# First head's values inside its forget product, an expert ring place released by halves, and one scatter moved ahead

## The chip, the core and the metric
The kernel runs on one core of a Trainium2 chip. The time is the device time of one execution in microseconds (us). TensorE (PE) multiplies; its weight loads (PEld) overlap its products. VectorE (DVE), ScalarE (ACT) and GpSimd (POOL) work elementwise, and SyncE (SP) issues most transfers. An engine takes its instructions strictly in the order written, and engines wait for one another on semaphores. PE runs at one of two clocks, 1.2 or 2.4 GHz.

## The reference
One inference layer for 256 prompt frames and 64 sample frames (T = 320 columns), width 1024:

```
x   = LN(x)
h @ w_in -> q, forget logits, values, output gate (8 heads of 128), conv branch, branch gates
logf = log_sigmoid(z) + log1p(lb * exp(-z));  k = (1 - lb) * sigmoid(-z)
S_t = diag(f_t) S_{t-1} + k_t v_t^T;  o_t = S_t^T q_t          per head, chunks of 64
A   = (rms_norm(o) * silu(g)) @ w_o_a
B   = silu(LN(causal depthwise conv(GLU))) @ w_o_b
x   = LN(alpha * x + (sig(ga) * A + sig(gb) * B) @ w_out)
y   = sum over 16 experts: gate_e * ((silu(x @ wg_e) * (x @ wu_e)) @ wd_e)   top 2 of one group of 4
out = LN(alpha * x + y)
```

The outputs are both y, and the new recurrent and conv states.

## The kernel before
**Start.** x is normalised, PE transposes it (L515) to 8 feature slices of 128 x 320 in PSUM. ACT and DVE turn each slice k into three things: xT (f32), a high part xh and a low part xl = xT - xh (both rounded for PE's faster f32 form). `X_COPIES` is DVE's order: "Tk" copies slice k to xT, "Lk" makes xl k. ACT walks k = 0 to 7: a slice that DVE copies needs one ACT instruction (L1108, xh from xT), any other needs two (L1111, L1112). A projection of one head is 24 products of 320 columns: weights high x xh, low x xh, high x xl. The weights' high part is made by ACT (`w_high`, L1076), the low part by DVE (`w_low`, L1568); POOL makes the very first one.

**Heads.** The mixer goes through 8 heads. In its turn each engine handles the current head and the one before it, in the order that its `head_turn` is written in. For the current head: PE makes the forget logits (`cur_f`, for head 0 `first_f`), q (`cur_q`) and values (`cur_v`, three `value_tile`s, plain f32: 24 products that stand as 48 in the trace). ACT runs the forget chain (L1123 to L1129), DVE the scan (L1591 to L1599). DVE and POOL then build 7 levels of decay differences (`level_decay` L1608, `key_decay` L1453), ACT exponentiates all of them in one instruction (`level_exp`, L1157), DVE and POOL multiply in q and k (L1621, L1467), and DVE ends with three small products; the last (L1635) is the decayed key. For the previous head: PE transposes that key (`prev_kT`, L596), makes the block products (`levels`, 64 x 64), the states and the output; DVE masks the block products (`level_mask`, L1644), which it does after the current head's scan and before the current head's level differences. Weights of head n + 2 go over those of head n; SP issues them when head n's values are done (semaphore v_done).

**Experts.** After the mixer x1 (320 rows) is routed. Experts are worked in 8 pairs; a pair has 12 groups of weights of 2 MB: 4 gate, 4 up, 4 down. SP streams them into a ring of 8 places (plus two groups, 11 and 23, kept elsewhere at first). A place is loaded again when PE has counted the old group done (`group_used`). `both` is one group: kk = 0, 1 by two halves of columns by two experts, 8 products of 512 columns (16 in the trace). The columns of a pair's tokens are gathered by PE: 3 products per feature slice (6 in the trace). For the first pair `first_gather(k)` does one slice k; ACT and DVE copy slices out two at a time (L1410, L2050: e.g. slices 0 and 1, semaphore eXT_a 1, and 2 and 3, eXT_b 1), and `first_gate(g)` is gate group g.

**End.** The last pair's down product is cut in quarters of 256 columns: `last_down(c)`, a copy by ACT (L1377), `last_scatter(c)` back to token rows in banks 0 to 2 (c even) or 3 to 5, and an add by DVE (L2067) with statistics (L2091). For the fourth quarter `last_sums` puts the running sum into the banks by PE, and DVE takes its statistics from PSUM (L2101). Then the last LayerNorm and the stores.

Of the kernel before, what the change touches and what calls it, by code (L numbers as in the profile page):

```python
# [25 lines left out]
P = 128  # L26
D = 1024
KT = D // P
# [54 lines left out]
    return c, np.stack(m, 1).reshape(P, LW).astype(np.float32)  # L83


X_COPIES = ("T1", "T3", "L0", "L1", "T6", "L2", "L3", "L4", "L5", "L6", "L7")
ORDER = [2, 0, 1]
X1_BANKS = [6, 7, 4, 5, 0, 1]
LOGIT_BANKS = [6, 7, 4]
# [32 lines left out]
def build(nc, a, o):  # L122
    with ExitStack() as ctx:
# [217 lines left out]
        def _(sp):  # L341
# [38 lines left out]
                sp.dma_start(sob[k], w_ob_k[:, k]).then_inc(wb_in, 16)  # L380
            with sp.Fori(1, 4) as i:
                for b in range(2):
                    sp.wait_ge(h["v_done"], 2 * i + b - 1)
                    load_head(i, b)
                    sp.wait_ge(h["so_ready"], 2 * i + b - 1)
                    sp.wait_ge(h["o_done"], 2 * i + b - 1)
                    load_state(i, b)
# [74 lines left out]
            load_extra(1, (2,))  # L462
            sp.wait_ge(logit_done, 3)
            load_extra(1, (3,))
            for g in range(SLOTS, 4 * PARTS):
                if g not in EXTRA:
                    load_first(g)
            with sp.Fori(2, PAIRS // 2 - 1) as i:
# [36 lines left out]
        def _(pe):  # L505
# [13 lines left out]
            def project(bank, hi, lo):  # L519
# [3 lines left out]
                        last = mm(ps[:, bank, 0:T], w[:, k * P:k * P + P], x[:, k, :], k == 0 and j == 0, k == KT - 1 and j == 2)  # L523
                return last

            def first_f():
                for k in range(KT):
# [4 lines left out]
                for k in range(KT):  # L532
                    pe.wait_ge(xl_ready, XL[k])
                    mm(ps[:, 0, 0:T], wh[:, k * P:k * P + P], xlk[:, k, :], False, False)
                pe.wait_ge(wlo_ready, 1)
                for k in range(KT):
                    last = mm(ps[:, 0, 0:T], wl[:, k * P:k * P + P], xhk[:, k, :], False, k == KT - 1)
                last.then_inc(h["f_done"], 1)

            def cur_f(i, b, first):  # L540
                pe.wait_ge(wlo_ready, 2 * (2 * i + b) + 1)
# [88 lines left out]
            def head_turn(cur, prev, pprev, first=False, first_prev=False):  # L630

                if first:
                    first_f()
                else:
                    cur_f(*cur, first)
                if first or first_prev:
                    cur_q(*cur, first, False)
                if first_prev:
                    prev_kT(*prev, True)
                    levels(*prev, True)  # L640
                    prev_states(*prev)
                if pprev:
                    rms(*pprev)
                    levels(*prev, False)
                    prev_kT(*prev, False)
                    cur_q(*cur, False, True)
                    prev_states(*prev)
                cur_v(*cur, first)
                if prev:
                    prev_out(*prev, first_prev)  # L650

# [177 lines left out]
            def both(bank, lhs, g, first=False):  # L829

                def weights(m, kk):
                    if first and g in EXTRA:
                        return extra[EXTRA.index(g)][2 * m + kk]
                    return wring[:, ring_place(g) % SLOTS if first else slot_of_group(g), m, kk, :]

                for kk in range(2):
                    k = 2 * (g % 4) + kk
                    for hf in range(2):
                        for m in range(2):
                            last = mm(ps[64 * m:64 * m + 64, bank + hf, :], lhs[:, k, 64 * m:64 * m + 64], weights(m, kk)[:, hf * 512:hf * 512 + 512],  # L840
                                      k == 0, k == KT - 1)
                return last

            def group(g, i, first=False):
                if first and g in EXTRA:
                    pe.wait_ge(extra_in[EXTRA.index(g)], 64)
                elif first:
                    pe.wait_ge(group_in[ring_place(g) % SLOTS], 16 * (ring_place(g) // SLOTS) + 16)
                else:
                    pe.wait_ge(group_in[slot_of_group(g)], 16 * (2 * PARTS // SLOTS) * i + 16 * ((g - len(EXTRA)) // SLOTS) + 16)  # L850
# [80 lines left out]
            def last_down(i, b, c):  # L931

                g = PARTS * b + 8 + c
                if c < 3:
                    group(g, i)
                else:
                    pe.wait_ge(e["end_in"], 16)
# [26 lines left out]
            def expert_pair(i, b, begin=False, end=False, first=False):  # L964
# [5 lines left out]
                if end:  # L970
# [30 lines left out]
            for k in range(5):  # L1001
# [4 lines left out]
            first_gather(5)  # L1006
            pe.wait_ge(e["eXT_b"], 1)
            first_gate(1)
            first_gather(6)
            first_gather(7)  # L1010
            pe.wait_ge(e["eXT_a"], 2)
            first_gate(2)
            pe.wait_ge(e["eXT_b"], 2)
# [28 lines left out]
        def _(act):  # L1042
# [172 lines left out]
            def head_turn(cur, nxt, prev, pprev, first=False, first_prev=False):  # L1215
                forget(*cur, first or first_prev)
                if pprev:
                    pprev_rms(*pprev)
                key_exp(*cur)
                if prev:  # L1220
                    prev_states(*prev, first_prev)
                if nxt:
                    w_high(*nxt, 0)
                else:
                    u_high(0, 0)
# [277 lines left out]
        def _(dve):  # L1503
# [170 lines left out]

            def head_turn(cur, nxt, prev, pprev, first=False, first_prev=False):
                forget_in(*cur, first or first_prev)
                if prev:
# [6 lines left out]
                if nxt:  # L1684
                    w_low(*nxt, 0)
                else:
                    u_low(0, 0)
# [314 lines left out]
            def last_hidden(n):  # L2002
                for hf in range(2):
                    cut = slice(hf * 512, hf * 512 + 512)
                    dve.wait_ge(e["group_used"] if hf else e["half_up"], PARTS * n + 8 if hf else 1)
# [156 lines left out]
```

## Time and profile before

| | |
|---|---|
| median of 3 runs | 870.38 us (869.27 to 871.08) |
| profiled execution, its own time | 869.76 us |
| span of that execution | 868.0 us |
| PE busy | 826.0 us, 95% |
| DVE / ACT / POOL busy | 412.5 / 238.2 / 80.0 us |
| HBM read | 247.99 MB |

The span runs from the first to the last instruction; 1.8 us of the execution's time lie around it. Engines share the span unevenly: DVE and ACT are densest in the heads (to about 200 us) and the conv (to about 300 us), while the transfers are saturated only in the expert part, from about 420 us on. A high busy share of PE is therefore no proof that PE sets the end.

### The profile page before, as it was taken

To read this page: it belongs to the slowest core of one execution; us is meant where nothing else is said; L and a number is where in the kernel's file an instruction comes from. 1 tells how busy PE (TensorE), PEld (TensorE's weight loads), DVE (VectorE), ACT (ScalarE), POOL (GpSimd) and SP (SyncE) were. 2 spreads that over 40 slices of the span, in tenths; PEclk is the share of its full clock that TensorE was granted. 3 is DMA by queue.
4 is the path that set the end of the run, shared out by engine and by line. 5 is a ranking of instruction groups with operands and counts; after the bars stand their busy time and mean duration, and the time that the engine had idled before them with its cause. 6 is when DMAs were issued, how large, how long until landed. Compare 5 with 4: busy or idle time off the path is not lost.

```text
span 868.0 us, 12770 instructions
## 1 busy us (share of the span) xinstructions
PE 826.0 (95%) x4976; PEld 536.6 (62%) x4976; DVE 412.5 (48%) x691; ACT 238.2 (27%) x377; POOL 80.0 (9%) x141
## 2 busy tenths in 40 slices
PE   4999999999999999999999999999999999999993
PEld 2989899989999867586353453543535335353351
DVE  6788889988999963876010302103021030210235
ACT  6666655665456415111101010000100001000011
POOL 1344455430000000000000000000000000000000
PEclk9999999999999999999999999999999999999997
DMA  8222222254343712499899999999999999999981
GB/s 317 74 83 84 82 82 82 106 181 148 145 146 123 318 45 103 185 400 413 327 429 430 426 429 427 427 428 427 427 428 430 428 427 430 425 431 424 430 362 62
DMA packets 32006, 251.07 MB, mean 289 GB/s; under 512 B 4638, under 2 KB 8094, under 8 KB 19674
## 3 DMA queue, kind: packets, MB, share of 16 engines
q1 hardware_dynamic: 29424, 249.17, 70.3%
q10 hardware_dynamic: 2538, 1.32, 0.5%
q8 instruction: 28, 0.46, 0.2%
q14 instruction: 16, 0.13, 0.0%
HBM read 247.99 MB, written 2.48 MB: 289 GB/s over the span
## 4 chain that ended last, share of the span: by engine, by line
PE 59%; DVE 21%; ACT 9%; DMA 8%; issue 2%; ACTq 1%; DVEq 0%
PE ps L507 58%; DVE ar L1730 5%; DMA ring<-in_w_down_end 4%; DMA ring<-in_w_gate_e 4%; DVE ring L1608 4%; DVE split_t L1737 3%; ACT ring L1157 2%; ACT ar L1167 1%; DVE ar L1644 1%; ACT split_w L1076 1%; DVE ar L1655 1%; DVE ar L1599 1%; PE ps L881 1%; ACTq L1206 1%; ACT ar L1129 1%
## 5 line engine op out<-in xcount | busy, mean ns | idle before, releaser
L507 PE MATMUL ps<-ring,ar 128*64 128x512 f32 (+1 forms) x1088 | 226.8, 568 | 4.3 <-ACT ar L1361 3.3
L507 PEld LDWEIGHTS ps<-ring,ar 128*64 128x64 f32 x1088 | 88.5, 137 | 130.3 <-issue 120.6
L507 PE MATMUL ps<-ring,xT 128*64 128x512 f32 (+2 forms) x896 | 161.1, 458 | 2.8 <-DMA ring<-in_w_gate_e 2.8
L507 PEld LDWEIGHTS ps<-ring,xT 128*64 128x64 f32 (+1 forms) x896 | 85.9, 152 | 72.8 <-issue 67.1
L2019 DVE TENSOR_TENSOR ar<-ar,ps 128x512 f32<-128x512 f32 (+1 forms) x42 | 28.8, 685 | 214.6 <-PE ps L507 214.5
L507 PE MATMUL ps<-split_x,split_t 128*128 128x320 f32 x672 | 101.0, 310 | 0.5 <-DVE split_t L1737 0.5
L507 PEld LDWEIGHTS ps<-split_x,split_t 128*128 128x128 f32 x672 | 98.6, 188 | 2.5 <-issue 1.4
L507 PE MATMUL ps<-split_x,split_w 128*128 128x320 f32 x480 | 79.4, 321 | 5.6 <-ACT ar L1212 1.7
L507 PE MATMUL ps<-ar 128*128 128x128 f32 (+7 forms) x340 | 80.1, 382 | 0.1
L507 PEld LDWEIGHTS ps<-split_x,split_w 128*128 128x128 f32 x480 | 72.8, 192 | 10.3 <-ACT split_x L1111 2.1
L1730 DVE SCALAR_TENSOR_TENSOR ar<-ar,params 128x350 f32<-128x350 f32 x116 | 67.7, 583 | 4.1
L507 PEld LDWEIGHTS ps<-ar 128*128 128x128 f32 (+2 forms) x340 | 39.4, 167 | 37.6 <-DVE ar L2019 19.5
L2000 DVE TENSOR_TENSOR ar<-ar,ps 128x1024 f32<-128x1024 f32 x7 | 8.5, 1221 | 88.5 <-PE ps L507 88.5
L507 PEld LDWEIGHTS ps<-ar,mid 128*128 128x128 f32 x384 | 43.7, 192 | 7.8 <-issue 7.8
L507 PE MATMUL ps<-ar,mid 128*128 128x128 f32 x384 | 45.4, 277 | 0.0
L507 PE MATMUL ps<-mid,ring 128*128 128x320 f32 x128 | 34.9, 432 | 0.0
L1453 POOL TENSOR_TENSOR ring<-ar 128x160 f32<-128x160 f32 (+1 forms) x56 | 28.3, 505 | 63.6 <-DVE ar L1599 59.8
L1373 ACT ACTIVATE ar<-ps 128x1024 f32<-128x1024 f32 x7 | 7.2, 1024 | 96.3 <-PE ps L507 96.3
L1467 POOL TENSOR_TENSOR ring<-ring,ar 128x160 f32<-128x160 f32 (+1 forms) x56 | 30.5, 544 | 25.5 <-ACT ring L1157 16.3
L1357 ACT ACTIVATE ar<-ps 128x1024 f32<-128x1024 f32 x8 | 8.2, 1024 | 89.4 <-PE ps L507 89.4
L1621 DVE TENSOR_TENSOR ring<-ring,ar 128x160 f32<-128x160 f32 (+1 forms) x56 | 30.5, 545 | 2.1 <-ACT ring L1157 0.2
L1608 DVE TENSOR_TENSOR ring<-ar 128x160 f32<-128x160 f32 (+1 forms) x56 | 30.2, 540 | 1.9
(220 smaller groups left out, 744.7 us busy)
## 6 DMA issues: line engine op xcount, KB each, us to landing
ring<-in_w_gate_e SPq DMA_DIRECT2D x32, 2048.0 KB, 16.5
ring<-in_w_up_e SPq DMA_DIRECT2D x32, 2048.0 KB, 17.3
ring<-in_w_down_e SPq DMA_DIRECT2D x26, 2048.0 KB, 19.7
ring<-in_w_in SPq DMA_DIRECT2D x56, 512.0 KB, 4.1
ring<-in_w_down_end SPq DMA_DIRECT2D x3, 2048.0 KB, 35.3
ring<-in_w_o_a SPq DMA_DIRECT2D x8, 512.0 KB, 5.7
ring<-in_w_out SPq DMA_DIRECT2D x1, 4096.0 KB, 14.7
ar<-in_w_down_e SPq DMA_DIRECT2D x6, 512.0 KB, 17.5
```

Of the source, the lines that this page charges most:

```text
L507: return pe.matmul(out, lhsT, rhs, start=start, stop=stop)
L881: last = pe.transpose(ps[:, k // 4, (k % 4) * P:(k % 4) * P + P], eh[:, k * P:k * P + P], ident)
L1076: signal(act, act.activation(piece(wh, q), sh[:, b, q].rearrange("p k n -> p (k n)"), ACT.Copy), whi_ready, 2 * n + q + 1)
L1129: signal(act, act.activation(hw, hw, ACT.Ln, scale=lb[:, bass.ds(n, 1)], bias=one1[:, :]), h["w_ready"], n + 1)
L1157: signal(act, act.activation(X[b], X[b], ACT.Exp), h["E_ready"], n + 1)
L1453: ins = pool.tensor_tensor(xv, bv[:, :, hs - 1:hs].to_broadcast([P, w // (2 * hs), hs]), bv[:, :, 0:hs], ALU.subtract)
L1467: ins = pool.tensor_tensor(xv, xv, kv, ALU.mult)
L1608: ins = dve.tensor_tensor(xv[:, :, hs:2 * hs], bv[:, :, hs:2 * hs], bv[:, :, hs - 1:hs].to_broadcast([P, w // (2 * hs), hs]), ALU.subtract)
L1621: ins = dve.tensor_tensor(xv, xv, qv, ALU.mult)
L1730: vc(dve.scalar_tensor_tensor(acc, uc[:, c, j:j + CW], vt[:, c, j:j + 1], acc, ALU.mult, ALU.add))
L1737: signal(dve, dve.tensor_tensor(t_lo[1 - b][q][1], stl[:, b, 8 * q:8 * q + 8].rearrange("p k n -> p (k n)"), t_hi[1 - b][q][0], ALU.subtract),
L2019: signal(dve, dve.tensor_tensor(yv, yv, ps[0:c, 4 + j % 2, :], ALU.add), e["y_added"], 6 * n + j + 1 + 6 * late)
```

## The change
1. X_COPIES: slices 5 and 7 are copied by DVE now, slice 6 no longer, so ACT has 12 instructions for the 8 slices in place of 13.
2. Head 0 on PE: `first_f` goes slice by slice, high and low weights by xh and, one slice late, high weights by xl. The 24 value products are put among them: those of slices 0 to 4 ahead of the last forget product, those of slices 5 to 7 behind it. All f_done and v_done signals follow, and q comes after both.
3. Head 1 on PE: its first value tile stands between the previous head's key transposes and its levels, the other two behind the states.
4. Head 0 on ACT and DVE: the next head's forget weights are split before key_exp (ACT) and before level_decay (DVE), not after.
5. SP: the loads of head n + 2 wait for q_done as well as v_done.
6. Experts: three slices are gathered ahead of gate group 0, not five; two ahead of group 1, three ahead of group 2. The first ring place is loaded again in two DMAs of 1 MB, the first when half of group 0 (kk = 0) is done.
7. End: `last_scatter(2)` stands ahead of `last_sums` and `last_down(3)`. end_in and half_up count one more from their new use.

```diff
-X_COPIES = ("T1", "T3", "L0", "L1", "T6", "L2", "L3", "L4", "L5", "L6", "L7")
+X_COPIES = ("T1", "T3", "L0", "L1", "T5", "L2", "L3", "T7", "L4", "L5", "L6", "L7")
@@ SP
+                    sp.wait_ge(h["q_done"], 2 * i + b - 1)
                     sp.wait_ge(h["v_done"], 2 * i + b - 1)
                     load_head(i, b)
...
+            sp.wait_ge(e["half_up"], 1)
+            sp.dma_start(wring[:, 0, :, 0, :], first_src[:, :, 0, :]).then_inc(e["end_in"], 16)
+            sp.wait_ge(e["group_used"], 1)
+            sp.dma_start(wring[:, 0, :, 1, :], first_src[:, :, 1, :]).then_inc(group_in[0], 16)
+            for g in range(SLOTS + 1, 4 * PARTS):
@@ PE, first_f
                 for k in range(KT):
...
                     mm(ps[:, 0, 0:T], wh[:, k * P:k * P + P], xhk[:, k, :], k == 0, False)
+                    mm(ps[:, 0, 0:T], wl[:, k * P:k * P + P], xhk[:, k, :], False, False)
+                    if k:
+                        pe.wait_ge(xl_ready, XL[k - 1])
+                        mm(ps[:, 0, 0:T], wh[:, (k - 1) * P:k * P], xlk[:, k - 1, :], False, False)
+                    if k == 4:
+                        pe.wait_ge(wh_in[0], 16)
+                        first_values(range(3))
+                    elif k > 4 and k < KT - 1:
+                        first_values((k - 2,))
...
+                first_values(range(KT - 3, KT)).then_inc(h["v_done"], 1)
@@ PE, head_turn
                 if first_prev:
                     prev_kT(*prev, True)
...
+                    value_tile(cur[1], 0)
                     levels(*prev, True)
                     prev_states(*prev)
+                    value_tile(cur[1], 1)
+                    value_tile(cur[1], 2).then_inc(h["v_done"], 1)
@@ PE, experts and end
+                    if first and g == 0 and kk == 0:
+                        last.then_inc(e["half_up"], 1)
...
                     last_scatter(1)
+                    last_scatter(2)
                     last_sums()
                     last_down(i, b, 3)
-                    last_scatter(2)
                     last_scatter(3)
@@ DVE (ACT alike, with w_high ahead of key_exp)
                 forget_in(*cur, first or first_prev)
+                if first:
+                    w_low(*nxt, 0)
...
                 level_decay(*cur)
```

On PE, at the second head, this stood in a row before (L596 the key transposes, `ps<-ring` and `ps<-ar` of 64 x 64 the levels, `ps<-ring,xT` the values; xk_ready and xr_ready come from POOL and DVE):

```order
L596 MATMUL ps<-cst,ar 128x128 [waits kdec_ready]
L596 MATMUL ps<-cst,ar 128x128
L596 MATMUL ps<-cst,ar 64x128
L507 MATMUL ps<-ring 64x64 [waits xk_ready,xr_ready]
L507 MATMUL ps<-ring 64x64 x11
```

Now 8 value products stand between the transposes and the levels:

```order
L620 MATMUL ps<-cst,ar 128x128 [waits kdec_ready]
L620 MATMUL ps<-cst,ar 128x128
L620 MATMUL ps<-cst,ar 64x128
L513 MATMUL ps<-ring,xT 128x128 [waits v_sb,wh_in1]
L513 MATMUL ps<-ring,xT 128x128 x7
L513 MATMUL ps<-ring 64x64 [waits xk_ready,xr_ready]
L513 MATMUL ps<-ring 64x64 x11
```

The row that waits for xk_ready and xr_ready has moved behind them. On DVE, in head 0's turn, from the scan on, before (L1608 the level differences, L1568 the low parts of weights):

```order
L1599 SCALAR_TENSOR_TENSOR ar<-cst,ar 128x320 [waits hc_dve]
L1608 TENSOR_TENSOR ring<-ar 128x2x64 [waits b_ready]
...
L1608 TENSOR_TENSOR ring<-ar 128x160 [waits hc_dve]
L1568 TENSOR_TENSOR split_w<-ring,split_w 128x1024 [waits whi_ready,dr_ready]
L1568 TENSOR_TENSOR split_w<-ring,split_w 128x1024 [waits whi_ready,wlo_ready]
L1621 TENSOR_TENSOR ring<-ring,ar 128x2x64 [waits q_sb,E_ready,wlo_ready]
```

and now:

```order
L1638 SCALAR_TENSOR_TENSOR ar<-cst,ar 128x320 [waits hc_dve]
L1607 TENSOR_TENSOR split_w<-ring,split_w 128x1024 [waits whi_ready,b_ready]
L1647 TENSOR_TENSOR ring<-ar 128x2x64 [waits wlo_ready]
...
L1647 TENSOR_TENSOR ring<-ar 128x160 [waits hc_dve]
L1607 TENSOR_TENSOR split_w<-ring,split_w 128x1024 [waits whi_ready,dr_ready]
L1660 TENSOR_TENSOR ring<-ring,ar 128x2x64 [waits q_sb,E_ready,wlo_ready]
```

One of the two weight splits went ahead of the seven level differences. On PE at the first expert pair (`ps<-ar,mid` the gather, 3 per slice; `ps<-ring,ar` a gate group), before:

```order
L507 MATMUL ps<-ar,mid 128x128 [waits pick_ready]
L507 MATMUL ps<-ar,mid 128x128 x14
L507 MATMUL ps<-ring,ar 64x512 [waits group_in0,eXT_a,routed]
L507 MATMUL ps<-ring,ar 64x512 x7
L507 MATMUL ps<-ar,mid 128x128 x3
L507 MATMUL ps<-ring,ar 64x512 [waits group_in1,eXT_b]
L507 MATMUL ps<-ring,ar 64x512 x7
L507 MATMUL ps<-ar,mid 128x128 x6
L507 MATMUL ps<-ring,ar 64x512 [waits group_in2,eXT_a]
```

and now:

```order
L513 MATMUL ps<-ar,mid 128x128 [waits pick_ready]
L513 MATMUL ps<-ar,mid 128x128 x8
L513 MATMUL ps<-ring,ar 64x512 [waits group_in0,eXT_a,routed]
L513 MATMUL ps<-ring,ar 64x512 x7
L513 MATMUL ps<-ar,mid 128x128 x6
L513 MATMUL ps<-ring,ar 64x512 [waits group_in1,eXT_b]
L513 MATMUL ps<-ring,ar 64x512 x7
L513 MATMUL ps<-ar,mid 128x128 x9
L513 MATMUL ps<-ring,ar 64x512 [waits group_in2,eXT_a]
```

The sum of gather products ahead of group 2 is the same, 24; six of them moved from ahead of group 0 to behind it.

## Rows read from the trace of the kernel before

**Rows 1.** The chain of waits, 25 to 66 us: start us, us, what

```profile
45.58 1.10 DVE ar L1644
...
52.50 2.03 ACT ring L1157
```

**Rows 2.** The chain of waits, whole span

```profile
798.13 35.41 DMA ring<-in_w_down_end
833.58 10.41 PE ps L507 x75
```

**Rows 3.** Timeline of PE, 0 to 75 us (start, us, what, count, [idle before <-releaser])

```profile
15.57 1.70 PE L507 MATMUL ps<-split_x,split_w 128*128 128x320 f32 x3 [0.79 <-ACT xT L1112]
...
20.89 8.25 PE L507 MATMUL ps<-split_x,split_w 128*128 128x320 f32 x42 [0.52 <-ACT split_x L1108]
28.98 5.63 PE L507 MATMUL ps<-ring,xT 128*128 128x128 f32 x48
35.84 7.30 PE L507 MATMUL ps<-split_x,split_w 128*128 128x320 f32 x48 [1.23 <-DVE split_w L1568]
...
43.40 0.92 PE L507 MATMUL ps<-ring 128*64 128x64 f32 x24
```

**Rows 4.** Timeline of PE, 21.9 to 24.3 us, then 25.4 to 28.9 us

```profile
21.54 3.03 PE L507 MATMUL ps<-split_x,split_w 128*128 128x320 f32 x10
...
25.17 3.97 PE L507 MATMUL ps<-split_x,split_w 128*128 128x320 f32 x26
```

**Rows 5.** Timeline of ACT, 0 to 62 us

```profile
21.52 0.62 ACT L1112 ACTIVATE xT<-ps,params 128x320 f32<-128x320 f32 x1
...
25.72 0.44 ACT L1123 ACTIVATE ar<-ps 128x320 f32<-128x320 f32 x1 [3.34 <-PE ps L507]
...
34.82 2.02 ACT L1157 ACTIVATE ring<-ring 128x2176 f32<-128x2176 f32 x1 [1.98 <-POOL ring L1453]
```

**Rows 6.** Timeline of DVE, 28 to 46 us

```profile
30.95 3.39 DVE L1608 TENSOR_TENSOR ring<-ar 128x128 f32<-128x128 f32 x7
34.38 2.66 DVE L1568 TENSOR_TENSOR split_w<-ring,split_w 128x1024 fp32r<-128x1024 f32 x2
37.07 4.34 DVE L1621 TENSOR_TENSOR ring<-ring,ar 128x128 f32<-128x128 f32 x7
...
42.18 0.49 DVE L1635 TENSOR_TENSOR ar<-ar 128x320 f32<-128x320 f32 x1
```

**Rows 7.** Stretches around 390 us: from:to, length, busy (x), PEclk granted, DMA

```profile
390.00:400.00 10.00, 9.24 (x47) 6.51 (x48) 6.11 (x16) 1.93 (x5) 0.00 (x0) 0.83 1.00 420
```

**Rows 8.** Timeline of PE, 408 to 430 us

```profile
408.74 3.51 PE L507 MATMUL ps<-ar,mid 128*128 128x128 f32 x30
412.18 3.65 PE L507 MATMUL ps<-ring,ar 128*64 128x512 f32 x16
```

**Rows 9.** Timeline of SP, 340 to 869 us: issues of ring weights

```profile
415.87 9.90 SPq L434 DMA_DIRECT2D ring<-in_w_down_e  x3
```

**Rows 10.** Line 434, issues at 415.9, 420.3 and 425.4 us

```profile
DMA to landing us min/median/max: 7.6/7.6/7.6
...
DMA to landing us min/median/max: 9.5/9.5/9.5
...
DMA to landing us min/median/max: 9.3/9.3/9.3
```

**Rows 11.** Stretches: last columns DMA share and GB/s

```profile
412.00:418.00 6.00, 6.00 (x33) 2.38 (x33) 0.11 (x1) 0.38 (x1) 0.00 (x0) 1.00 0.52 154
```

**Rows 12.** Timelines of PE, then DVE, 832 to 856 us

```profile
844.56 1.70 PE L507 MATMUL ps<-ar,cst 128*128 128x256 f32 x6 [0.57 <-DVE ar L2067]
...
849.79 3.34 PE L507 MATMUL ps<-ar 128*128 128x256 f32 x12
...
850.60 1.42 DVE L2067 TENSOR_TENSOR ar<-ar,ps 128x256 f32<-128x256 f32 x3 [4.72 <-PE ps L507]
...
853.43 0.43 DVE L2101 BATCH_NORM_STATS2 ar<-ps 128x6 f32<-128x256 f32 x1
```

More of the change, by code:

```diff
@@ L464, in _ @@
             load_extra(1, (3,))
-            for g in range(SLOTS, 4 * PARTS):
+            first_src = column(experts[SLOTS % PARTS // 4], SLOTS % 4).rearrange("p (m k n) -> p m k n", m=2, k=2)
+            sp.wait_ge(e["half_up"], 1)
[3 more added lines that the diff above has]
+            for g in range(SLOTS + 1, 4 * PARTS):
                 if g not in EXTRA:
@@ L524, in project, with first_values @@
                 return last
+            def first_values(ks):
+                for k in ks:
+                    if k in XT_D:
+                        pe.wait_ge(xl_ready, XT_D[k])
+                    else:
+                        pe.wait_ge(xh_ready, XT_A[k])
+                    for t in (0, 2, 1):
+                        t0, n = TILES[t]
+                        last = mm(ps[0:n, 3, t * P:t * P + P], xT[:, k, t0:t0 + n], sh[:, 0, 3, k, :], k == 0 and t == 0, k == KT - 1 and t == 1)
+                return last
             def first_f():
+                pe.wait_ge(wlo_ready, 1)
                 for k in range(KT):
@@ L531, in first_f @@
                     mm(ps[:, 0, 0:T], wh[:, k * P:k * P + P], xhk[:, k, :], k == 0, False)
[L532 to L538, printed above, removed]
+                    mm(ps[:, 0, 0:T], wl[:, k * P:k * P + P], xhk[:, k, :], False, False)
[7 more added lines that the diff above has]
+                        first_values((k - 2,))
+                k = KT - 1
+                pe.wait_ge(xl_ready, XL[k])
+                mm(ps[:, 0, 0:T], wh[:, k * P:k * P + P], xlk[:, k, :], False, True).then_inc(h["f_done"], 1)
+                first_values(range(KT - 3, KT)).then_inc(h["v_done"], 1)
             def cur_f(i, b, first):
@@ L647, in head_turn @@
                     prev_states(*prev)
-                cur_v(*cur, first)
+                if not first and not first_prev:
+                    cur_v(*cur, first)
                 if prev:
@@ L847, in group @@
                 elif first:
+                    if g == SLOTS:
+                        pe.wait_ge(e["end_in"], 16)
                     pe.wait_ge(group_in[ring_place(g) % SLOTS], 16 * (ring_place(g) // SLOTS) + 16)
@@ L936, in last_down @@
                 else:
-                    pe.wait_ge(e["end_in"], 16)
+                    pe.wait_ge(e["end_in"], 32)
                 if c >= 2:
@@ L1000, in _ @@
             pe.wait_ge(e["pick_ready"], 1)
-            for k in range(5):
+            for k in range(3):
                 first_gather(k)
@@ L1005, in _ @@
             first_gate(0)
-            first_gather(5)
+            first_gather(3)
+            first_gather(4)
             pe.wait_ge(e["eXT_b"], 1)
             first_gate(1)
-            first_gather(6)
-            first_gather(7)
+            for k in range(5, KT):
+                first_gather(k)
             pe.wait_ge(e["eXT_a"], 2)
@@ L1218, in head_turn @@
                     pprev_rms(*pprev)
+                if first:
+                    w_high(*nxt, 0)
                 key_exp(*cur)
@@ L1221, in head_turn @@
                     prev_states(*prev, first_prev)
-                if nxt:
+                if first:
+                    pass
+                elif nxt:
                     w_high(*nxt, 0)
@@ L1676, in head_turn @@
                 forget_in(*cur, first or first_prev)
+                if first:
+                    w_low(*nxt, 0)
                 if prev:
@@ L1683, in head_turn @@
                     pprev_out(*pprev)
-                if nxt:
+                if first:
+                    pass
+                elif nxt:
                     w_low(*nxt, 0)
@@ L2004, in last_hidden @@
                     cut = slice(hf * 512, hf * 512 + 512)
-                    dve.wait_ge(e["group_used"] if hf else e["half_up"], PARTS * n + 8 if hf else 1)
+                    dve.wait_ge(e["group_used"] if hf else e["half_up"], PARTS * n + 8 if hf else 2)
                     dve.wait_ge(e["silu_ready"], n + 1)
```

2 lines of the change are left out of this document (added).

## The prediction
> **What bounds the kernel now.** I read the chain of waits first. Early in the program it runs through DVE and ACT, not PE: the mask of head 0's block products at 45.58 us and the exponential of head 1's levels at 52.50 are on it [rows 1], and pieces like these repeat head by head, so a delay at 45.58 reaches everything behind it. Late it is a transfer until 833.58 and PE after that [rows 2]: the expert weights arrive as one unbroken stream, and the end is the landing of the second quarter of the last down weights plus a fixed tail. So three places count: head 0 and 1 up to the mask, the start of the expert stream, and the tail. I go through them in this order, with the timelines of PE, ACT and DVE. Between head 1 and the expert part nothing is changed, and I carry a shift through it undiminished, since the chain has no wait for a transfer there. If the mixer is early or late, the stream starts as much early or late.
>
> **Head 0, when the forget logits are done.** Call F the moment at which ACT reads them: 25.72 now, after 3.34 us of waiting for PE [rows 5]. The split of x ends earlier with the new copies: one of ACT's 0.62 us instructions goes [rows 5], and a DVE copy of about that size enters, where DVE stood idle between slices. The last low part is then ready at about 22.0, not 22.7. That isn't what decides; PE is. PE starts at 15.57 and has now three short stalls before 20.89 [rows 3], in which the new order puts real work, but 15 of the 24 value products also come ahead of F. A value product is two entries of 5.63/48 = 0.117 us, a slice 0.70 us, five slices 3.5 us [rows 3]. PE's clock decides the rest. The rows show it at its lower level until some time past 24: ten forget products take 3.03 us there, and from 25.17 on 26 of the same shape take 3.97 [rows 4], so 0.27 to 0.30 each against 0.15. Before it rose PE had worked without a stall from 20.89, for some 3.6 us. In the new order it works without one of note from 15.57. By slices: 14 products at the slow rate, paced by x, reach 19.5. If the clock is up by then, what remains is 10 products at 0.15 and 3.5 us of values: 24.5, plus 0.4 until ACT starts, F = 24.8 with a small allowance. If it rises at 21.1, F is 25.3; if it rises only at 24.5 as it does now, 18 of the value entries cost twice as much and F is 26.9. If it is up by 17.7, F is 24.1. I take 24.8, a gain of 0.9, with ends of +1.6 and -1.2. The nearest row for the time a rise takes is the 3.6 us above, which from 15.57 gives 19.2.
>
> The Trainium skill ("TensorE: Matmul & The Clock Gate", section "What's actually happening") says that the monitor behind the gate runs free and doesn't start with the kernel, so that the moment of the rise varies from run to run. No row here can show that, there being one trace; by it, F of both kernels would scatter, which is a reason for the width above and changes no term.
>
> **Head 0, the split of head 1's weights.** It moves ahead of the level differences. The first of the two splits takes about half of 2.66 us, the differences 3.39 [rows 6]. Now the one exponential starts at 34.82, released by POOL [rows 5]; DVE's own differences end 0.5 earlier. With the split first DVE ends them at 30.95 + 1.25 + 3.39 = 35.6, perhaps 0.3 less since the last two no longer run beside POOL. The exponential is 0.6 to 0.8 late. The second split still hides under it, and L1621, which now starts at 37.07 behind both splits, starts 0.5 late (0.4 to 0.75). What is gained is head 1's forget product, 3 us earlier than 35.84 [rows 3], but ACT gets to it only after its exponentials, which are late, and DVE's queue is full until the decayed key: nothing there waits for PE. ACT's half of the edit, 1.06 us, hides in ACT's wait.
>
> **Head 1, a value tile ahead of the levels.** The decayed key (42.18 + 0.49 = 42.67, [rows 6]) releases the key transposes and, right behind, the levels at 43.40 [rows 3]; the mask follows 2.18 later, at 45.58 [rows 1]. In the new order 8 value products, 16 entries or 1.9 us, stand in between, and PE can't pass them. PE will be idle ahead of the transposes, for some 3 us, since both projections of head 1 are done early; that idle time isn't used, because the tile stands behind the transposes. Key ready at 42.67 + 0.5 = 43.2, transposes to 43.65, values to 45.55, levels: 2.15 later than 43.40. The mask of head 0 is 2.2 late against F (1.9 to 2.5), and DVE has nothing else to do there. What goes from behind the levels, 5.63 - 1.9 us, gives nothing back: head 1's values are read by ACT only after the exponential of 52.50. Behind SP's new wait for q_done stand the loads of heads 2 and on, which ACT wants 20 us later: zero. Head part: 2.2 - 0.9 = **+1.3**, between +0.5 and +3.6.
>
> **The expert stream.** A gather slice is 3.51/5 = 0.70, a group 3.65 [rows 8]. Group 0 starts at 412.18 now, and at 410.9 with two slices less ahead of it; ACT's copy of the first two slices is ready then to 0.1. The first refill is issued at 415.87 [rows 9]; during 412 to 418 the transfers are busy only 52% [rows 11]. New: half a group after 410.9 the first megabyte is issued, at 412.9, the second at 414.6. Landings now: 415.87 + 7.6 = 423.5, 420.3 + 9.5 = 429.8, 425.4 + 9.3 = 434.7, [rows 9, 10]; the last two are 4.9 apart, which is the stream's pace. So 1.4 us are lost between the first and the second, besides the gap. New: first refill landed at 420.5. Group 1 starts at 415.9 in place of 416.6, and its refill goes out at 419.5. Group 2 starts when it does now, since 24 gather products and two groups are ahead of it as before, and the third refill goes out at 425.3. That is the catch: from there a lone transfer needs 7.6, landing at 432.9, and one that meets another's tail 9.3, landing at 434.6. The stream gains between 0.1 and 1.8 for a place that is 3 us early. From the fourth refill on PE is ahead of the stream. I take **-0.7**, the middle, as both rows are equally near. The end waits for the stream, so this arrives in full.
>
> [...]
>
> **The tail.** The third scatter stood behind the last down product. PE has 0.57 of idle time ahead of the sums at 844.56, and spends 3.34 on two scatters from 849.79 [rows 12]. DVE adds the third quarter at 850.60 and takes its statistics until 853.43, when the fourth quarter's begin [rows 12]; DVE sets the pace there. New: the third scatter fills 843.85 to 845.25, and sums and last product come 0.7 later, ending at 850.5; ACT's copy of the fourth quarter then stands open, 0.6, and its scatter gives DVE the first tile at 852.0. The adds and statistics of the third quarter are long done. 853.43 - 852.0 = **-1.4** (-1.0 to -1.5). The last weights land by 843, well ahead. ACT's table load is done by 852.4, hidden.
>
> **Sum.** +1.3 - 0.7 - 1.4 = -0.8, against the profiled execution's own 869.76: 869.0. That execution lies 0.6 below the median of 870.38; laid on the median the sum is 869.6. I state 869.3, between them.
>
> **Rivals.** (a) The clock of PE is up before 18 and the third refill lands like a lone transfer. For it: PE is busy from 15.57; against it: products starting at 15.57 were never followed by a rise before 24 in this trace. F gains 1.6, the stream 1.5: 2.2 - 1.6 - 1.5 - 1.4 = -2.3, 867.7. (b) Slower: the 3 us of idle time ahead of head 1's key transposes lower the clock. For it: around 390 us, where PE has little but waits and tiny products, the granted clock falls (0.83 over ten microseconds, [rows 7]). Against it: PE idles 1.23 us ahead of 35.84 [rows 3], and the products behind that run at the full rate (48 in 7.30). The tile then costs 3.4 and not 1.9, the levels behind it up to 0.8 more, all on the path: +2.3 on the sum, 871.6. It decides once more than 0.8 of it is real. The same section of the Trainium skill says that idle time lowers the gate again, which speaks for this rival; the time is the one above. (c) The clock rises late, as it does now, F = 26.9: +2.1 on the sum, 871.3. (d) The levels aren't pushed, because something else holds the mask: against it stands that the mask starts 2.18 behind the first of them, about as long as they take (24 of 60 entries in 0.92, [rows 3]); without the push the sum is -2.7, 867.2.
>
> **Chances.** Forecast 0.50 (own range 868.4 to 870.8), (a) 0.20, (b) 0.12, (c) 0.13, (d) 0.05. Range 867.4 to 871.9: it leaves out the far parts of (a) and (d) below and of (b) and (c) together above. What a measurement here tells from no change is about 0.2%, 1.7 us. Faster than that: (a), (d) and a fifth of the forecast's case, 0.33. Slower than that: (b) and (c) only where both meet or the stream gives nothing, 0.12. Within: 0.55.
>
> **What would show it.** Right: F at 24.5 to 25.3; the first exponential of the levels at about 35.5 + (F - 25.7); PE idle some 3 us ahead of the key transposes, then 16 entries of values, and DVE idle about 2 us ahead of the mask, which starts near 47; the first refill in two issues about 3 us early against the gather's start, the third at most 0.2 early; the fourth quarter's statistics directly behind its scatter. Wrong: a mask at 45.6 or earlier, an F above 26, PE's granted clock below full around 43 us, or a third refill issued a microsecond early.

## The result and the profile after
The changed kernel takes 871.80 us (median of 20 runs, 869.50 to 873.38), the kernel before 870.23 (20 runs, 868.99 to 871.76): ratio 1.0017, 95% interval 1.0009 to 1.0024, so 0.8 to 2.1 us slower. The forecast was 869.3, a small gain. A second series gave 871.13 and 1.0013 (1.0004 to 1.0022).

F is that of the prediction; the rows below the first are moments, counted from the start of the span.

| profiled execution | before | after |
|---|---|---|
| its own time, span | 869.76, 868.0 | 872.09, 870.2 |
| F | 25.72 | 26.25 |
| mask of head 0 | 45.58 | 48.48 |
| levels' exponential of head 1 | 52.50 | 54.74 |
| gather starts | 408.74 | 413.15 |
| PE goes on behind the last awaited landing | 833.58 | 837.02 |
| DVE's statistics, fourth quarter | 853.43 | 855.64 |

The changed kernel is 2.2 us late at the exponential, 4.4 at the gather, 3.4 at the landing and 2.2 at the end. Head 0 on PE (columns as in rows 3, to be read against them; an "entry" below is one of the counted lines of the trace, and a value product has two):

```profile
15.72 3.96 PE L513 MATMUL ps<-split_x,split_w 128*128 128x320 f32 x14 [1.09 <-ACT xT L1147]
19.52 3.17 PE L513 MATMUL ps<-ring,xT 128*128 128x128 f32 x18
22.44 0.69 PE L513 MATMUL ps<-split_x,split_w 128*128 128x320 f32 x3
22.97 1.16 PE L513 MATMUL ps<-ring,xT 128*128 128x128 f32 x6
23.89 0.69 PE L513 MATMUL ps<-split_x,split_w 128*128 128x320 f32 x3
...
25.33 0.83 PE L513 MATMUL ps<-split_x,split_w 128*128 128x320 f32 x4
...
44.03 0.55 PE L620 MATMUL ps<-cst,ar 128*128 128x128 f32 x3 [2.61 <-DVE ar L1674]
44.41 1.95 PE L513 MATMUL ps<-ring,xT 128*128 128x128 f32 x16
46.29 0.92 PE L513 MATMUL ps<-ring 128*64 128x64 f32 x24
```

No stall is left between 15.72 and F. Three forget products and a slice of values take 23.89 - 22.44 = 1.45 us; at 0.15 each for the three, a slice costs 1.00, where rows 3 gave 0.70. On the timeline of ACT, the read of the forget logits and the exponential of head 0's levels, against rows 5:

```profile
26.25 0.44 ACT L1158 ACTIVATE ar<-ps 128x320 f32<-128x320 f32 x1 [4.53 <-PE ps L513]
...
36.41 2.02 ACT L1192 ACTIVATE ring<-ring 128x2176 f32<-128x2176 f32 x1 [2.10 <-DVE ring L1647]
```

DVE at head 0's mask, against the row on the chain [rows 1]; it waits 2.07 us for PE:

```profile
48.48 1.09 DVE L1683 TENSOR_TENSOR ar<-ps,mid 128x896 f32<-128x896 f32 x1 [2.07 <-PE ps L513]
```

Behind the start, two stretches of this execution show PE's clock at its lower level: near 183 us, where the trace of before has none, and near 394 us, where it has a shorter one [rows 7]. I call such a stretch a fall of the clock. Views by stretch, columns as in rows 7 (PEclk is the third from the end):

```profile
183.00:186.60 3.60, 3.60 (x62) 3.60 (x59) 0.87 (x1) 0.75 (x2) 0.00 (x0) 0.53 0.07 19
390.00:402.00 12.00, 12.00 (x63) 8.91 (x61) 5.80 (x13) 2.23 (x5) 0.00 (x0) 0.72 1.01 418
412.00:418.00 6.00, 6.00 (x36) 3.67 (x38) 1.43 (x7) 0.38 (x1) 0.00 (x0) 1.00 0.90 362
```

The last one is the stretch of rows 11, but the gather starts 4.4 us later here. The stretch that lies as far behind the gather as that of rows 11, 416.41 to 422.41 us, has the transfers busy 78%, against 52%. SP's issues against rows 9 (first half, second half, then two refills):

```profile
417.23 0.62 SPq L468 DMA_DIRECT2D ring<-in_w_down_e  x1
418.95 0.55 SPq L470 DMA_DIRECT2D ring<-in_w_down_e  x1
424.07 6.12 SPq L435 DMA_DIRECT2D ring<-in_w_down_e  x2
```

From issue to landing, at the lines of the first half, the second and the two refills:

```profile
DMA to landing us min/median/max: 4.9/4.9/4.9
...
DMA to landing us min/median/max: 7.3/7.3/7.3
...
DMA to landing us min/median/max: 7.7/7.7/7.8
```

The tail of the changed kernel, PE (against rows 12):

```profile
845.71 3.34 PE L513 MATMUL ps<-ar 128*128 128x256 f32 x12
848.99 1.70 PE L513 MATMUL ps<-ar,cst 128*128 128x256 f32 x6
850.62 3.67 PE L513 MATMUL ps<-ring,ar 128*64 128x256 f32 x32
854.84 1.71 PE L513 MATMUL ps<-ar 128*128 128x256 f32 x6 [0.54 <-ACT ar L1416]
```

### The profile page after: what moved, and what is told of

It reads as the page before. It is cut to its first block, busy times and chain, and to the rows that moved or that the text cites. A ratio compares the mean times of both kernels' runs of the same rounds, so it can differ in the third digit from the quotient of the medians.

```text
span 870.2 us, 12780 instructions
## 1 busy us (share of the span) xinstructions
PE 828.3 (95%) x4976; PEld 538.4 (62%) x4976; DVE 412.3 (47%) x692; ACT 237.2 (27%) x376; POOL 80.5 (9%) x141
## 4 chain that ended last, share of the span: by engine, by line
PE 63%; DVE 21%; ACT 8%; DMA 5%; issue 2%; ACTq 1%; DVEq 0%; SPq 0%
PE ps L513 62%; DVE ar L1773 5%; DMA ring<-in_w_down_end 4%; DVE ring L1647 4%; DVE split_t L1780 3%; ACT ring L1192 2%; DVE ar L1683 1%; DVE ring L1660 1%; ACT ar L1202 1%; ACT split_w L1111 1%; PE ps L915 1%; DVE ar L1694 1%; DVE ar L1638 1%; DMA ar<-in_x_prompt 1%; DVE ring L1556 1%
## 5 line engine op out<-in xcount | busy, mean ns | idle before, releaser
L513 PE MATMUL ps<-ring,xT 128*64 128x512 f32 (+2 forms) x896 | 164.1, 459 | 2.0 <-DMA ring<-in_w_gate_e 2.0
L513 PEld LDWEIGHTS ps<-ar 128*128 128x128 f32 (+2 forms) x340 | 39.7, 169 | 38.3 <-DVE ar L2062 19.5
L1660 DVE TENSOR_TENSOR ring<-ring,ar 128x160 f32<-128x160 f32 (+1 forms) x56 | 29.9, 534 | 2.9 <-ACT ring L1192 1.1
## 6 DMA issues: line engine op xcount, KB each, us to landing
ring<-in_w_down_e SPq DMA_DIRECT2D x25, 2048.0 KB, 19.2
ring<-in_w_out SPq DMA_DIRECT2D x1, 4096.0 KB, 14.7
```

Source lines behind the costliest of these rows:

```text
L513: return pe.matmul(out, lhsT, rhs, start=start, stop=stop)
L1660: ins = dve.tensor_tensor(xv, xv, qv, ALU.mult)
```

## The experiments
Each ratio is to runs of the kernel before that were made beside it. "Against F" takes the moment at which ACT reads head 0's forget logits as zero, which removes what differs ahead of it. The mask is 19.86 us behind F before and 22.23 after.

### What made F late
**d_vals**: all values behind the last forget product.

```diff
-                        first_values(range(3))
...
-                        first_values((k - 2,))
...
-                first_values(range(KT - 3, KT)).then_inc(h["v_done"], 1)
+                pe.wait_ge(wh_in[0], 16)
+                value_tile(0, 0)
+                value_tile(0, 1)
+                value_tile(0, 2).then_inc(h["v_done"], 1)
```

> The changed kernel with all of head 0's value products behind its last forget product, tile by tile, and none among them. Theory (the values are what keeps F late, since the last low part of x is ready at 22.1 us): F at 22.8 us in place of 26.25, the mask at about 45.1 in place of 48.5, 3.4 us faster. Rival (without them PE stalls between slices, and its clock rises late, as in the kernel before): F at 24.5 to 25.7 us, 0.6 to 1.7 us faster. The 48 value entries take 5.6 us again, if it is their order that makes them dearer in the changed kernel.

867.01 us, ratio 0.9966 (0.9954 to 0.9979), 4.1 to 4.8 below the changed kernel's two medians, where 3.4 was expected. F is at 22.39, mask at 45.20, and the clock rose at 19.6 without the values' help. The 48 entries take 5.63 us again:

```profile
15.43 5.38 PE L513 MATMUL ps<-split_x,split_w 128*128 128x320 f32 x20 [1.09 <-ACT xT L1145]
21.26 1.03 PE L513 MATMUL ps<-split_x,split_w 128*128 128x320 f32 x4 [0.45 <-ACT split_x L1141]
22.13 5.63 PE L513 MATMUL ps<-ring,xT 128*128 128x128 f32 x48
```

So the values were all that kept F at 26, and their order is what made them dear. The slice order goes from a tile of 128 rows to one of 64 and back in every slice; by tiles that happens once.

**e_width**: only the 128-row tiles among the forget products.

```diff
-                    for t in (0, 2, 1):
+                    for t in (0, 1):
...
+                for k in range(KT):
+                    mm(ps[0:n, 3, 2 * P:3 * P], xT[:, k, t0:t0 + n], sh[:, 0, 3, k, :], False, False)
                 first_values(range(KT - 3, KT)).then_inc(h["v_done"], 1)
```

> The changed kernel with only the two tiles of 128 rows of each slice's values among the forget products; the third tile, of 64 rows, follows for all eight slices behind F, so that PE switches once to stationary blocks of 64 columns and not once a slice. Theory (each such switch costs, 0.33 us a slice there and back): a slice of values costs 0.45 us ahead of F, F at 26.25 - 5 x (1.00 - 0.45) = 23.5 us, the mask 2.7 us earlier, of which 1.1 is work moved behind F. Rival (each change of the place in PSUM costs, whatever the width): a slice costs 0.65 or more, F at 24.5 or later.

868.46 us, 0.9976 (0.9963 to 0.9990); F is at 23.84. Its PE timeline:

```profile
21.13 0.69 PE L513 MATMUL ps<-split_x,split_w 128*128 128x320 f32 x3
21.66 0.60 PE L513 MATMUL ps<-ring,xT 128*128 128x128 f32 x4
22.02 0.69 PE L513 MATMUL ps<-split_x,split_w 128*128 128x320 f32 x3
```

A slice of four entries costs 22.02 - 21.13 - 0.45 = 0.44 us, 0.11 an entry, though each product goes to another place in PSUM. The rival is out. A tile of x is the stationary operand here, so its rows are columns of the stationary block: going from blocks of 128 columns to one of 64 and back costs 1.00 - 6 x 0.11 = 0.34 us a slice. (F was 0.3 above my number; the clock rose at 20.4 in this trace, not at 19.3.)

**j_f**: the good half of it alone, on the kernel before: forget product by slices and the new copies, q and values as before (the line of X_COPIES as in the change).

```diff
...
                     mm(ps[:, 0, 0:T], wh[:, k * P:k * P + P], xhk[:, k, :], k == 0, False)
+                    mm(ps[:, 0, 0:T], wl[:, k * P:k * P + P], xhk[:, k, :], False, False)
+                    if k:
+                        pe.wait_ge(xl_ready, XL[k - 1])
+                        mm(ps[:, 0, 0:T], wh[:, (k - 1) * P:k * P], xlk[:, k - 1, :], False, False)
```

> The kernel before with the forget product of head 0 slice by slice and the new copies of x, nothing else: q and the values follow as before. Theory: F at 22.4 us, all of the 3.3 us reach the end: 867.0. With the 1.0 of the stream and the 1.2 of the tail that makes 5.5 of the 6.3 us that the combined kernel gained. Rival (part of the gain is kept only because the stream starts early): 868 or more.

867.02 us, 0.9965 (0.9951 to 0.9978), F at 22.49, mask at 42.34. As expected.

### Head 1
**c_tile**: the value tile ahead of the key transposes.

```diff
-                    prev_kT(*prev, True)
...
                     value_tile(cur[1], 0)
+                    prev_kT(*prev, True)
                     levels(*prev, True)
```

> The changed kernel with head 1's first value tile ahead of the key transposes instead of behind them. Theory (PE idles 2.6 us there and the tile pushes the levels): the tile fits in the idle time, the levels follow the transposes at once, the mask of head 0 starts at about 46.6 us in place of 48.5, the whole kernel is 1.8 us faster. Rival (the mask is late because DVE's or POOL's work is, and PE only looks like it): mask at 48.5, no change.

868.73 us, 0.9982 (0.9972 to 0.9992), 2.4 to 3.1 below the changed kernel's two medians. The mask is at F + 20.46, 1.77 earlier, and DVE waits 0.28 for it, not 2.07. That is more time than the mask explains. Its trace has no fall of the clock between the start and the end, and the idle time that the tile now fills is the one in which the clock falls in other traces (below); that this is the rest is likely, but not shown by this run.

**f_split**: the weight splits of head 1 back behind the exponential and the level differences (ACT alike).

```diff
...
                 forget_in(*cur, first or first_prev)
-                if first:
-                    w_low(*nxt, 0)
```

> The changed kernel with head 1's weight splits where they were (behind the exponentials on ACT, behind the level differences on DVE). Theory: the exponential of head 0's levels starts 0.6 to 1.2 us earlier against F (it is 10.2 us behind F in the changed kernel, 9.1 before), the decayed key 0.5 earlier; but the forget product of head 1 waits for its low part until 35 us, so PE reaches the transposes at 43.0 instead of idling: mask 0.4 earlier against F, the time 0.3 to 0.5 us below the changed kernel's. Rival (the splits were neutral where they are now): mask at F + 22.2 as now.

872.32 us, 1.0021 (1.0010 to 1.0032): not faster, against my expectation. The exponential is 1.08 earlier against F (9.08, not 10.16), as expected. But PE now waits for the low part:

```profile
38.00 8.84 PE L513 MATMUL ps<-split_x,split_w 128*128 128x320 f32 x48 [3.66 <-DVE split_w L1603]
```

Forty-eight such products take 7.3 us in rows 3; behind 3.66 us of idle time they take 8.84, since the clock is low from 39.2 to 42.6, and the mask is at F + 23.17. (F itself is 27.90 in this trace, with a start 0.7 late and the clock up only at 22.2.) In this trace the clock gave back what the order had gained; the median lies 0.5 to 1.2 above the changed kernel's, which one trace doesn't explain.

### The clock
**after_again**: the changed kernel unchanged.

> The changed kernel once more, unchanged. Theory (its times fall into two groups, 869.5 to 870.7 and 871.6 to 873.4, by whether PE's granted clock falls to its lower level behind 181.8 us and how long it does near 394): two groups again, some 2.3 us apart, median between 870.5 and 872.2; the trace of a run of the lower group shows the levels behind 182 us in 4.6 us, not 6.1. Rival (the spread is the stream's and has nothing to do with the clock): one broad group, and a low time with the clock fall in its trace.

871.13 us, 869.94 to 872.82. Over both series 16 of 32 runs are above 871.5. The two groups that I expected aren't there: 870.94, 870.98 and 871.28 lie between them. This trace (time 870.94) has no fall near 183, as expected of a low time, but one that I hadn't expected, at the end of the 2.6 us of idle time ahead of head 0's key transposes:

```profile
44.25 0.90 PE L620 MATMUL ps<-cst,ar 128*128 128x128 f32 x3 [2.63 <-DVE ar L1674]
44.95 3.11 PE L513 MATMUL ps<-ring,xT 128*128 128x128 f32 x16
47.98 0.92 PE L513 MATMUL ps<-ring 128*64 128x64 f32 x24
```

The stretches at that place and near 183 (columns as in rows 7):

```profile
43.90:47.40 3.50, 3.15 (x15) 3.12 (x16) 2.59 (x5) 1.97 (x4) 0.55 (x2) 0.51 0.00 0
183.00:186.60 3.60, 3.08 (x70) 2.68 (x71) 1.54 (x3) 1.37 (x3) 0.00 (x0) 1.00 0.28 93
```

The tile takes 3.11 in place of 1.95, and DVE starts the mask at F + 23.73, 1.5 later than in the first trace:

```profile
50.17 1.09 DVE L1683 TENSOR_TENSOR ar<-ps,mid 128x896 f32<-128x896 f32 x1 [3.54 <-PE ps L513]
```

**k_fill43**: work in that idle time, into a bank that the levels write afresh.

```diff
                 if first_prev:
+                    for _ in range(16):
+                        mm(ps[:, LEVEL_BANKS[0], 0:T], xhk[:, 0, 0:P], xhk[:, 0, :], True, True)
                     prev_kT(*prev, True)
```

> The changed kernel with 16 products of 320 columns ahead of the previous head's key transposes, in PE's idle time of 2.6 us (2.4 us of work, into a bank that the levels write afresh). The value tile still stands behind the transposes. Theory (the idle time lowers the clock in some runs, in others not): the mask is at 48.5 in every run and never at 49.7 to 50.2, since the clock doesn't fall near 43.5 us; median 0.5 to 0.9 us below the changed kernel's 871.1 to 871.8. Rival (the clock falls there because of the thin products behind, idle or not): times as those of the changed kernel.

870.68 us (868.51 to 870.88, 11 runs), 1.0002 (0.9993 to 1.0011). The mask is at F + 22.27, the clock stays up there, and none of the 11 times is above 870.9, where 16 of 32 were above 871.5. By the median the gain is 0.5 to 1.1 us, and the intervals of the ratios (1.0009 to 1.0024 and 1.0004 to 1.0022 without the work) overlap a little; what shows the effect is the missing upper times. With l_fills, below, 1 of 23 runs with this idle time filled is above 871.5, while f_split, run beside both, has 6 of 10 there. So useless work there makes the kernel faster: the idle time lowered the clock, not the thin products behind it. The profiled execution, at 870.88 the slowest of the 11, has the fall at 183.5.

**g_fill**: the same ahead of the last head's levels, 10 products.

```diff
+            pe.wait_ge(ulo_ready, 1)
+            for _ in range(10):
+                mm(ps[:, U_BANKS[0][0], 0:T], u_hi[0][0][1][:, 0:P], xhk[:, 0, :], True, True)
             conv_value(0)
             rms(3, 0)
```

> The changed kernel with 10 more products of 320 columns ahead of the conv's first value product (they only overwrite a bank that is written afresh behind them), so that PE doesn't idle 1.76 us ahead of the last head's levels. They cost no time, as PE waits for ACT there. Theory (the idle time lowers the clock behind it in some runs): no fall of the clock at 183 us, the upper group of times gone or nearer by 1.5 us: median 0.8 us below the changed kernel's in the same call. Rival (the thin products of the levels lower it, idle or not, or another cause): as the changed kernel.

870.78 us (868.06 to 873.04, 12 runs), 1.0003 (0.9991 to 1.0014). No fall near 183 in its trace, but that near 43 is there (tile 2.92, mask at F + 23.53), and two times are above 872. The median is 0.35 below that of after_again, where 0.8 was expected. Near 183 the clock falls in five of the twelve traces in which PE idles 1.8 us there, and in neither of the two in which it doesn't (g_fill, l_fills): that the idle time is the cause there too isn't shown.

**l_fills**: both of these edits.

> Both fillings together, that ahead of head 0's key transposes and that ahead of the last head's levels. Theory: the clock falls neither near 43.5 nor near 183 us, what remains is the fall near 394 us; the times lie in one group near 869.5 to 870.3, median 1 to 1.8 us below the changed kernel's. Rival: as the changed kernel, 870 to 873.

870.65 us (868.37 to 871.56, 12 runs), 1.0002. No fall anywhere in its trace until the end. But the median is that of k_fill43 and above the 869.3 to 870.3 that I expected, and the times still lie 3.2 us apart: the second filling brought nothing that 12 runs can tell, and falls at these two places aren't all of the scatter. That trace started its first product at 16.76, 1.0 to 1.5 us later than all others but f_split, a scatter of the start that no edit explains.

What a fall costs, by the traces: near 183, from the first product of the group to the key transposes, 186.85 - 181.77 = 5.08 us in the changed kernel's first trace and 187.05 - 183.52 = 3.53 in its second, so 1.55. Near 394, from the second set of router products to the third, 5.63 with no fall (l_fills), 6.13 and 6.89 with one of 3.4 us (after_again, before), 7.41 with one of 6.8 us (the first trace).

All fourteen traces bear this out between head 1's exponential and the start of the gather. No version compared here adds work to the path there:

| falls of the clock in between | traces | us |
|---|---|---|
| none | c_tile, f_split, l_fills, h_best | 354.9 to 355.0 |
| near 394 | a_tail, b_expert, after_again, g_fill | 355.3 to 355.5 |
| near 394 | before | 356.2 |
| near 177 (j_f), 181 (e_width) | j_f, e_width | 356.4, 356.5 |
| near 180 or 183, and near 394 | d_vals, k_fill43 | 356.9 |
| near 183, and near 394 for twice as long | after | 358.4 |

Without a fall this part of the program repeats within 0.15 us, with falls it is 0.3 to 3.5 us longer. So falls account for the 2.2 us by which the traces of before and after differ there.

### Stream and tail
**b_expert** and **a_tail**: these parts of the change alone, on the kernel before (of b_expert's edit one piece is shown, the rest is as in point 6 of the change).

```diff
-            for k in range(5):
+            for k in range(3):
                 first_gather(k)
```

```diff
                     last_scatter(1)
+                    last_scatter(2)
                     last_sums()
                     last_down(i, b, 3)
-                    last_scatter(2)
```

> The kernel before with the expert part of the change alone: three slices gathered ahead of group 0, the first ring place loaded in two halves. Theory: the stream gains 1.0 us from the start of the gather to the landing that PE waits for last; 869.2. Rival A (each later refill keeps its distance to PE, the early refill is hidden): 870.2. Rival B (the third refill lands like a lone transfer): 1.8 us, 868.4.

> The kernel before with the third scatter moved ahead of the sums and of the fourth down product, nothing else. Theory (the parts add up; the tail's part was worth what the two traces show between PE's start behind the second quarter's weights and the fourth quarter's statistics, 1.2 us): 1.2 us faster, about 869.0, and DVE's statistics of the fourth quarter start 1.2 us earlier against PE's start behind that landing than in the kernel before. Rival (the tail was earlier in the changed kernel only because its last weights lay ready longer): no change, 870.2.

b_expert: 868.70 us, 0.9979 (0.9970 to 0.9989). a_tail: 868.59, 0.9980 (0.9970 to 0.9991). Both intervals contain what was expected, that of b_expert also the 1.8 us of rival B: its median is 1.7 below, so the run doesn't tell the two apart. The tail's part is exact in every trace: from PE's start behind the awaited landing to DVE's statistics, 19.85 us in the three with the old tail, 18.62 or 18.63 in the eleven with the new. The stream's is not: from the gather's start to that landing there are 424.84, 425.15 and 425.80 us in the three traces with the old start, and 423.74 to 425.79, mean 424.36, in the eleven with the new. The means differ by 0.9 us, and the traces of one kind scatter by more than that, so one trace can't size it.

### What to keep
**h_best**: the kernel before with the three edits of j_f, b_expert and a_tail.

> What seems worth keeping: the kernel before with the forget product of head 0 slice by slice (the new copies of x with it), no value product ahead of F, head 1 and both weight splits as before, and the expert and tail parts of the change. Theory: F at 22.4 us as without values among the products, everything behind shifted by 3.3 us as far as the mask (about 42.3 us in a run whose mask was at 45.6 before), stream 1.0 and tail 1.2 earlier: 5.5 us faster than before, 864.9. Rival (PE in head 1 becomes late in its place, since its 48 products wait for the weights' low parts): mask at 43.5 or later, 866.2 or more.

864.04 us (863.33 to 864.51, 5 runs), ratio 0.9928 (0.9915 to 0.9941), so 5.1 to 7.4 us faster than before. F at 22.43, mask at 42.29, no fall of the clock. It is the fastest of the kernels, and its five times lie within 1.2 us.

## Why the prediction was wrong, step by step
The time lies in the stated range, but on the slower side of no change, where a gain was forecast.

**F.** The step that failed: "A value product is two entries of 5.63/48 = 0.117 us, a slice 0.70 us, five slices 3.5 us". In the slice order a slice costs 1.00, five cost 5.0, and F is 26.25, not 24.8; these 1.5 us are the whole miss of F, and "an F above 26" was among the signs of being wrong. The 5.63 were measured on a row with one switch of width, the new code has two in each slice. The 14 products reach 19.52 (19.5). The clock was up at 19.3 (19.2), but so near a hit was luck: in the eleven traces with the slice order it rose at 18.8 to 22.2, 3.3 to 5.7 us behind the first product. Against the two other traces that keep the old start (F at 26.27 and 26.37) the change of F is nothing, where a gain of 0.9 was forecast. (Two small slips change nothing: 24.5 + 0.4 is 24.9, and the chances of a faster kernel add up to 0.35.)

**Weight split first.** The exponential is 1.06 late against F (0.6 to 0.8 forecast), the decayed key 0.77 (0.5). DVE's differences took 3.60, not 3.39 or less. L1660 started 0.92 late (0.5 forecast), but took 3.89 (4.34 before, [rows 6]).

**Value tile.** Right: mask 2.37 late against F (2.2), PE idle 2.61 ahead of the transposes (3), DVE 2.07 (2). That the push is the tile's c_tile shows. The head part in this trace is +2.24 (+1.3). The difference is F, 1.4, and 0.2 at the mask, less 0.66 that DVE made good between the mask and head 1's exponential, where two of its steps were shorter than before; the prediction had carried the mask's delay on in full. On the timeline of DVE before, then now:

```profile
47.36 1.04 DVE L1655 TENSOR_TENSOR ar<-ar 128x576 f32<-128x576 f32 x1
48.43 3.99 DVE L1608 TENSOR_TENSOR ring<-ar 128x128 f32<-128x128 f32 x7
...
50.26 0.76 DVE L1694 TENSOR_TENSOR ar<-ar 128x576 f32<-128x576 f32 x1
51.05 3.61 DVE L1647 TENSOR_TENSOR ring<-ar 128x128 f32<-128x128 f32 x7
```

Why they were shorter no run shows.

**Rival (b)** was given 0.12, against it that the clock stood 1.23 us of idle time in rows 3. It is real in some executions: two of the three traces with that code and no filling (after_again, g_fill) have it, two other kernels that idle 2.25 and 2.61 us there (d_vals, e_width) don't in theirs, and k_fill43 removes it. Its price is 1.3 to 1.5, not 2.3, since only the tile meets it and the levels don't. Carrying the shift "undiminished" from head 1 to the experts failed likewise: this trace adds 2.2 there by falls of the clock, some 1.5 near 183 and the rest near 394, where before had a fall too. The Trainium skill ("TensorE: Matmul & The Clock Gate", section "What's actually happening") says that idle time lowers the gate and that the monitor runs free of the kernel. The traces agree: with the same code the clock fell near 183 in one and near 44 in another. I had named the first for this rival, but used the free monitor for the rise alone.

**Stream.** The first refill was issued 3.05 us early against the gather (3), the third at the same distance. The first was whole only 13.1 us behind the gather's start (11.8 forecast, 14.7 before), since its second half took 7.3. The third landed like a lone transfer (7.7), as rival (a) had it, 1.5 us early; at the end 0.9 is left (0.7), by the means of the traces.

**Tail.** It gained 1.23 (1.4), by the mechanism described; the scatter is released at 854.84 by ACT's copy after 0.54 of idle time (0.6).

**The sum.** In this pair of traces head +2.2, stream -1.0 and tail -1.2 make nothing, where -0.8 was forecast, and the falls of the clock behind head 1 make +2.2. Over all runs, by the medians, it is +0.8 to +1.6. So the sign was wrong because F gained nothing, and falls of the clock, for which the sum had no term, added to it. That these occur in some runs only, at three places, for 0.5 to 1.8 us, is shown; how often each occurs isn't, since only profiled executions show the clock.

## What to carry to other kernels
A price per entry holds for the order it was measured in: before interleaving products, count how often the width of the stationary block changes. Don't put work on PE behind a wait when PE idles ahead of that wait; ahead of it, it was free here, and it kept the clock up. Split a change that combines several ideas: here the forget product by slices, the earlier refill and the earlier scatter are worth 5 to 7 us together, and the others cost that and more.

## What the runs showed of the hardware
- Switching from stationary blocks of 128 columns to 64 and back costs 0.34 us (plain f32, 128 moving columns, clock at its higher level); a change of the place in PSUM costs nothing.
- Idle times of PE of 1.8, 2.6 and 3.7 us came with a lower granted clock in some executions, the first two not in others (the third was seen once). A fall cost 0.5 us at the cheapest place.
- With 16 useless products in an idle time of 2.6 us the highest of 11 times was 870.9, without them that of 32 was 873.4.
